# Where a one-core transformer kernel computes a convolution's filter, splits its weights and turns its heads: a rearranged instruction order on one Trainium2 core

## The reference

```python
for l in range(DEPTH):
    xn = rmsnorm(x, norm_mix[l])
    # a: chunked attention with a relative bias; b: difference of two softmaxes;
    # c: attention to the keys that an indexer picks (top_k of its scores)
    y = g[:, :, 0] * (o_a @ w_up_a[l]) + g[:, :, 1] * (o_b @ w_up_b[l]) + g[:, :, 2] * (o_c @ w_up_c[l])
    x = x + y @ w_out[l]
    x = x + memory_cross_attention(rmsnorm(x, norm_cross[l]), mem_n, w_q_x[l], w_kv_x[l], w_o_x[l])
    x = x + swiglu(rmsnorm(x, norm_ffn[l]), w_gu[l], w_down[l])
```

```python
def hyena_filter(length, fw1, fb1, fw2, fb2, fw3, fb3, fw4, freq):
    h = jnp.sin(freq * (emb @ fw1 + fb1))
    h = jnp.sin(freq * (h @ fw2 + fb2))
    h = jnp.sin(freq * (h @ fw3 + fb3))
    h = (h @ fw4).astype(jnp.float32)
    h_fwd = h[:, :HY_WIDTH] * window
    h_bwd = h[:, HY_WIDTH:] * window
```

## Time and profile before

| | us |
|---|---|
| runs, median (lowest to highest) | 3005.87 (3005.4 to 3010.86) |
| the profiled execution | 2997.0 |
| its span | 2995.2 |
| PE busy in it | 2914.2 (97%) |
| VectorE (DVE) busy | 1969.0 (66%) |
| ScalarE (ACT) busy | 1273.9 (43%) |
| GpSimd (POOL) busy | 226.4 (8%) |
| mean granted clock of TensorE | 0.991 |

### The profile page before, as it was taken

The page is one execution under the profiler, slowest core; times in us unless marked ns, Lnnn a source line. Parts: engine busy times, 40 slices in busy tenths (PEclk is TensorE's granted clock), DMA queues, the critical chain, the costliest instruction groups (busy, mean ns, idle before and its releaser), DMA issues.

```text
span 2995.2 us, 55989 instructions
## 1 busy us (share of the span) xinstructions
PE 2914.2 (97%) x23366; PEld 2765.4 (92%) x23366; DVE 1969.0 (66%) x3288; ACT 1273.9 (43%) x2199; POOL 226.4 (8%) x304
## 2 busy tenths in 40 slices
PE   8999899999999999999999999999999998999999
PEld 7889799988998999999977899999999998887899
DVE  6676688567768867767586666665666655335655
ACT  4455554445555463222545352223522234235543
POOL 1311100132101000000011200000000001001000
PEclk9999999999999999999999999999999999999999
DMA  6435377543546745554231234444345443342464
GB/s 210 132 121 173 121 246 236 173 126 110 169 145 207 247 159 197 183 180 157 93 109 43 75 113 162 151 143 138 127 162 168 142 144 97 113 148 92 148 197 135
DMA packets 246240, 448.49 MB, mean 150 GB/s; under 512 B 14739, under 2 KB 88356, under 8 KB 245348
## 3 DMA queue, kind: packets, MB, share of 16 engines
q1 hardware_dynamic: 239072, 430.79, 44.5%
q10 hardware_dynamic: 6916, 14.12, 1.4%
HBM read 442.75 MB, written 1.05 MB: 148 GB/s over the span
## 4 chain that ended last, share of the span: by engine, by line
PE 86%; DVE 8%; ACT 4%; issue 2%; POOL 0%; DMA 0%; ACTq 0%; SPq 0%; DVEq 0%; POOLq 0%
PE ps L1390 67%; DVE split L2202 3%; PE ps L1468 2%; PE ps L1469 2%; PE ps L1470 2%; ACT split L1876 1%; PE ps L1575 1%; PE ps L1340 1%; DVE A L2199 1%; PE ps L1764 1%; PE ps L1290 1%; PE ps L1599 1%; ACT A L1926 1%; ACT AR L1923 1%; DVE AR L2202 1%
## 5 line engine op out<-in xcount | busy, mean ns | idle before, releaser
L1390 PE MATMUL ps<-AR,split 128*128 128x256 f32 x18528 | 2211.4, 280 | 20.7 <-POOL AR L2762 5.3
L1390 PEld LDWEIGHTS ps<-AR,split 128*128 128x128 f32 x18528 | 2158.7, 189 | 64.0 <-issue 30.8
L2202 DVE TENSOR_TENSOR split<-raw,split 128x1024 fp32r<-128x1024 f32 (+2 forms) x728 | 810.0, 1150 | 546.6 <-ACT split L1876 540.1
L1876 ACT ACTIVATE split<-raw 128x1024 fp32r<-128x1024 f32 (+2 forms) x728 | 686.7, 987 | 761.9 <-PE ps L1390 670.0
L2487 DVE SCALAR_TENSOR_TENSOR junk<-A,cb 128x1024 bf16<-128x1024 f32 x144 | 175.6, 1220 | 42.0 <-DMA A<-w_modT 39.3
L2202 DVE TENSOR_TENSOR AR<-A,AR 128x256 fp32r<-128x256 f32 (+2 forms) x292 | 144.7, 496 | 48.7 <-ACT A L1926 25.8
L2487 DVE SCALAR_TENSOR_TENSOR A<-A,cb 128x1024 f32<-128x1024 f32 x144 | 175.3, 1218 | 0.0
L2755 POOL TENSOR_TENSOR A<-A 128x256 f32<-128x256 f32 x54 | 41.0, 759 | 1586.4 <-ACT A L1895 1583.4
L1948 ACT ACTIVATE AR<-A 128x256 fp32r<-128x256 f32 (+1 forms) x132 | 68.4, 526 | 193.4 <-DVE A L2326 193.4
L2199 DVE SCALAR_TENSOR_TENSOR A<-A,ps 128x256 f32<-128x256 f32 (+1 forms) x196 | 95.0, 505 | 49.3 <-ACT A L1944 44.7
L1944 ACT ACTIVATE A<-ps 128x256 f32<-128x256 f32 (+1 forms) x132 | 62.6, 490 | 128.4 <-PE ps L1390 125.8
(11 more groups left out here) (267 smaller groups left out, 2525.0 us busy)
## 6 DMA issues: line engine op xcount, KB each, us to landing
A<-w_modT SPq DMA_DIRECT2D x144, 512.0 KB, 4.5
raw<-w_in SPq DMA_DIRECT2D x120, 512.0 KB, 4.3
raw<-w_gu SPq DMA_DIRECT2D x80, 512.0 KB, 4.8
raw<-ffn_a_in SPq DMA_DIRECT2D x80, 512.0 KB, 4.5
raw<-ffn_b_in SPq DMA_DIRECT2D x80, 512.0 KB, 4.5
raw<-ret_in SPq DMA_DIRECT2D x48, 512.0 KB, 4.4
raw<-w_down SPq DMA_DIRECT2D x44, 512.0 KB, 4.7
raw<-ffn_a_out SPq DMA_DIRECT2D x44, 512.0 KB, 4.4
```

What stands on the lines that cost most here:

```text
L1390: mm = e.matmul(out[:, s:s + NT], wt[:, c, m_], xs(k0 + c, a + s, a + s + NT), start=first and part + s == 0, stop=last and part == 2 and ...
L1876: e.activation(hi, self.raw_view(q), ACT.Copy).then_inc(*self.mark(("w hi", q)))
L2202: return self.e.tensor_tensor(out, v, hi.bitcast(F32), ALU.subtract)
```

## The change

It moves work in the walk, and changes a few waits and banks:

- The start: VectorE no longer waits for x at first (`await_inputs` does it after the first norm's sums), its first half of a weight is split after the reciprocal, 14 warm-up matmul calls for 8, single halves prepared behind chunks 1, 3 and 5.
- The indexer of layer 0 takes PSUM banks 4, 6, 7, 0 in place of 0, 1, 2, 3.
- The fence before the first attention becomes `await_first`, which waits for the banks of q, k and v of attention a; the wait for the second attention's values moves from `await_second` to the first `diff_values`.
- In the cross attention weights are split at side steps 2 and 3 (not 4 and 6), the split at step 7 is dropped, and the root table is loaded at step 4.
- The silu of c is made in two halves in layer 0's output projection.
- The filter network: its loads go into layer 0's gate product, its three layers and sines into layer 0's down product, its taps and VectorE's end into the norm behind and layer 1's start, the products of its transform into layer 1's feed-forward norm and down product. The even stage keeps none of it.
- The retention: the second half of q's parts (m > 3) is exchanged by DMA as k's are; weights for it are split at steps 5 and 6 of the crossing, and the context's chunks start at step 7 and not 5.
- In an attention pipeline, put-off halves are no longer split in the rounds in which no new unit starts and at most two are live.

```diff
@@ pipeline
-                if put_off:
+                if put_off and (new or parts > 2):
                     self.split_beside(at, parts)
@@ cross_steps
-            if c == 3 and early:
-                self.prepare(AHEAD, True)
+            if c == 3:
+                self.prepare_beside()
+            if early and c in (5, 6):
+                self.prepare(AHEAD, c == 5)
                 self.asked -= 1
-            elif c == 3:
-                self.prepare_beside()
...
-            if c > 4:
+            if c > (6 if early else 4):
                 next(ctx)
@@ walk, the start
-        self.prepare_first()
-        self.warm(8)
+        if self.name != "dve":
+            self.prepare_first()
+        self.warm(14)
         self.norm_sums(n0)
+        if self.name == "dve":
+            self.prepare_first()
+        self.await_inputs()
@@
-then=lambda c: c in (2, 4) and self.prepare_behind(c // 2 - 1))
+then=lambda c: c in (1, 3, 5) and self.prepare_behind(c // 3, c == 3))
@@ layer_one, after the cross attention
+        if l == 1:
+            self.filter_product(0, 0)
         self.next_sums(nf, 0)
+        if l == 1:
+            self.filter_product(0, 1)
...
-            if n == 12 and l == 0:
-                self.mod_start()
+            if l == 0 and n < 96 and n % 16 == 12:
+                self.load_filter(n // 16)
@@ layer_one, down
+            if l == 0 and k in (0, 5, 10):
+                self.filter_layer(k // 5)
+            if l == 0 and k in (4, 9, 14):
+                self.filter_sine(k // 5)
+            if l == 1 and k == 2:
+                self.filter_product(1, 0)
+                self.filter_product(1, 1)
+            if l == 1 and k == 3:
+                self.filter_spectra(1)
         if l == 0:
             h = self.H1("h mix 1")
-            self.next_norm(nn, self.xl, h, gain=self.cl("norm_mix", 8, 8))
+            self.filter_tap("forward", 0, 6)
+            self.next_sums(nn, 1)
+            self.filter_tap("backward", 0, 7)
+            self.norm_spread(nn["name"], [nn])
+            self.filter_tap("forward", 1, 4)
+            h.norm = nn["name"]
+            self.norm_apply(nn, self.xl, h, gain=self.cl("norm_mix", 8, 8))
+            self.filter_end(0)
@@ beside_cross
+            if k in (2, 3):
+                self.prepare(0, k == 2)
+                self.asked -= 1
             if k == 4:
                 self.await_memory_values(l)
-            if k in (4, 6):
-                self.prepare(0, k == 4)
-                self.asked -= 1
-            if k == 5:
                 self.load_roots()
-            if k == 7:
-                self.prepare_beside(True)
@@ mixing
-        run(first_a, self.indexer(...))
+        run(first_a)
+        if l == 1:
+            self.filter_tap("backward", 1, 6)
+            self.filter_end(1)
+        run(self.indexer(...))
...
-        self.fence()
-        self.fence(("act",))
+        self.await_first(l)
@@ the output projection
+            if l == 0 and k in (1, 9):
+                self.mod_start(k // 8)
@@ odd
-self.project_t("q r", w, 0, 1024, h, lambda m, f: self.axial(..., m, rawb, tmpb), ...)
+self.project_t("q r", w, 0, 1024, h, lambda m, f: self.axial(..., m, rawb, tmpb, moved=m > 3), ...)
@@ TensorE.indexer
-        waits = [self.K.take(f, PROJ) for f in fills]
+        waits = [self.K.take(f, (4, 6, 7, 0) if l == 0 else PROJ) for f in fills]
@@ TensorE
+    def await_first(self, l):
+        for m in range(4):
+            for v in ("qa", "ka"):
+                self.e.wait_ge(*self.after(("free", ((v, l), m))))
+        for m in range(2):
+            self.e.wait_ge(*self.after(("free", (("va", l), 0, m))))
+
+    def filter_product(self, kind, m):
+        f = (("even", "odd")[m], "filter spectrum", kind)
+        out = self.fresh(f, (6 + m,))
+        self.e.wait_ge(*self.after("fdft"))
+        self.e.wait_ge(*self.after(("filter taps", m)))
+        o = FDFT + kind * 256 + m * P
+        self.e.matmul(out[:, :], self.A[:, o:o + P], self.taps(2 * kind + m), start=True, stop=True).then_inc(*self.mark(("full", f)))
@@ ScalarE.axial
-        if ctx is not None:
+        if moved:
             e.wait_ge(*self.after(("raw", f)))
             e.dma_start(dst[0:64, :], raw[64:128, :])...
             e.dma_start(dst[64:128, :], raw[0:64, :])...
```

More of the change, by code:

```diff
@@ L589, in first_block @@
         h.norm = "first"
-        self.norm_apply(n0, self.xl, h, self.cl("norm_mix", 0, 8), then=lambda c: c in (2, 4) and self.prepare_behind(c // 2 - 1))
+        self.norm_apply(n0, self.xl, h, self.cl("norm_mix", 0, 8), then=lambda c: c in (1, 3, 5) and self.prepare_behind(c // 3, c == 3))
         self.await_tables()
@@ L606, in first_block, with prepare_behind @@
         return h
-    def prepare_behind(self, ahead):
-        self.prepare(ahead)
+    def prepare_behind(self, ahead, part):
+        self.prepare(ahead, part)
         self.asked -= 1
@@ L740, in context_norm @@
             yield
+        yield
         self.norm_sums(N)
@@ L1001, in hyena_spectra @@
         for kind in range(2):
-            self.filter_spectra(kind)
-            yield
-        for kind in range(2):
             self.spectra(0, kind)
@@ L1257, in nothing @@
         pass
[L1259 removed]
+    start = finish = await_inputs = warm = split_memory = await_tables = prepare_first = norm_feed = norm_sums = norm_spread = keep = add_x_out = add_mod_out = add_set_out = nothing
     silu = gated = gated_low = gate = up = rotary = index_twice = index_weights = index_score = nothing
@@ L1623, in await_second @@
             self.e.wait_ge(*self.after(("rotated", ((v, l), 3))))
-        for m in range(2):
-            self.e.wait_ge(*self.after(("free", (("vb", l), 0, m))))
     def diff_values(self, name, pt, nk, vs, o, ptb, kt):
@@ L1629, in diff_values @@
         out = self.fresh(f, BESIDE[2])[:, 0:P]
+        if name[2] == name[3] == 0:
+            for m in range(2):
+                self.e.wait_ge(*self.after(("free", (("vb", name[1]), 0, m))))
         self.e.wait_ge(*self.after(("pt", name)))
@@ L1710, in forward @@
             self.e.matmul(out[:, :], self.A[:, o:o + P], src(m), start=True, stop=True).then_inc(*self.mark(("full", (part, *f))))
-    def filter_spectra(self, kind):
-        self.e.wait_ge(*self.after("dft"))
-        self.forward(("filter spectrum", kind), lambda m: self.taps(2 * kind + m), kind, lambda m: ("filter taps", m))
     def spectra(self, s, kind):
         ZT = 18432
+        if s == kind == 0:
+            self.e.wait_ge(*self.after("dft"))
         self.forward(("spectrum", kind, s), lambda m: self.A[:, ZT + (2 * s + m) * 512:ZT + (2 * s + m + 1) * 512], kind, lambda m: ("free", ("z turn", 2 * s + m)))
@@ L1830, in load_lambda @@
     def load_lambda(self, l):
+        if l == 1:
+            self.e.wait_ge(*self.after(("filter taps", 1)))
         if l == 0:
@@ L2063, in await_projected @@
         self.e.wait_ge(*self.after(rsb.freed(7)))
-        self.e.wait_ge(*self.after(("filter taps", 1)))
     def normed(self, f, dst, gain, sqb, rsb):
@@ L2095, in filter_spectra @@
     def filter_spectra(self, kind):
-        self.keep(("even", "filter spectrum", kind), self.A[:, HS + (2 * kind + 1) * 512:HS + (2 * kind + 2) * 512], 1)
+        self.keep(("even", "filter spectrum", kind), self.taps(2 * kind), 1)
     def spectra(self, s, kind):
@@ L2116, in axial @@
         raw = self.A[:, o:o + NT]
-        e.activation(raw, self.bank(f)[:, 0:NT], ACT.Copy, scale=scale).then_inc(*self.mark(("raw", f), *([("free", f)] if ctx is not None else [])))
-        if ctx is not None:
+        e.activation(raw, self.bank(f)[:, 0:NT], ACT.Copy, scale=scale).then_inc(*self.mark(("raw", f), *([("free", f)] if moved else [])))
+        if moved:
             e.wait_ge(*self.after(("raw", f)))
@@ L2187, in start, with await_inputs @@
     def start(self):
-        for v in ("cols", "eps", "x0", "x1", "x2", "x3"):
+        for v in ("cols", "eps"):
+            self.e.wait_ge(*self.after(v))
+    def await_inputs(self):
+        for v in ("x0", "x1", "x2", "x3"):
             self.e.wait_ge(*self.after(v))
@@ L2589, in filter_spectra @@
     def filter_spectra(self, kind):
-        self.both_halves(("filter spectrum", kind), kind, HS + 2 * kind * 512)
+        e, f = self.e, ("filter spectrum", kind)
+        low, high, odd = self.taps(2 * kind), self.taps(2 * kind + 1), self.bank(("odd", *f))[:, :]
+        e.wait_ge(*self.after(("free", ("even", *f))))
+        e.wait_ge(*self.after(("full", ("odd", *f))))
+        if kind == 0:
+            e.tensor_tensor(high, low, odd, ALU.subtract).then_inc(*self.mark(("frequencies", f, 1)))
+        else:
+            e.tensor_tensor(high, odd, low, ALU.subtract).then_inc(*self.mark(("frequencies", f, 1)))
+        e.tensor_tensor(low, odd, low, ALU.add).then_inc(*self.mark(("free", ("odd", *f)), ("frequencies", f, 0)))
     def spectra(self, s, kind):
-        self.both_halves(("spectrum", kind, s), kind, ZS[s] + 2 * kind * 512)
```

(2 more changed lines are left out.)

158 lines of the change are left out of this document (72 added, 86 removed).

## The result

| | before | after |
|---|---|---|
| median of 10 runs (lowest to highest), us | 3008.97 (2998.41 to 3022.84) | 2992.48 (2972.42 to 3000.16) |
| ratio to before | | 0.9933, 95% interval 0.9907 to 0.9959 |
| the profiled execution's span, us | 2995.2 | 2995.8 |
| granted clock, mean | 0.991 | 0.989 |

In these runs the change is faster, by 20 us of 3009 as the ratio goes (12 to 28), where 29.5 were forecast; 2992.5 lies in the range of 2957 to 2994, near its upper end. The two profiled executions show no difference at all. So the first question is what hides it there.

A forecast was written before the change was run, and what follows sets the result against it. PE, busy 2914.2 of 2995.2 us, was taken as the bound, with gains only in its waits and half clock. Terms summed to -31.5, with +2 for new waits -29.5: 3005.87 to 2976 us, range 2957 to 2994.

The forecast's parts named there:

- rival 1: Whole kernel: waits are displaced, each term gives only its low end, -3.5 us, half of that way -12; chance 0.11.
- F: Layer 0's gate product: moving the silu of c to the output projection removes PE's 3.4 us wait, -2.9 us.
- G: Filter network: the even stage loses 13.3 us on PE, 6.1 come back elsewhere, -7.2 us.
- H: Start of the retention layer: earlier weight splits and half of q's parts turned by DMA, -8 us.
- E: Cross attention's tail, both layers: earlier splits and one dropped shorten PE's waits for POOL, -4.4 us.
- A, B: Kernel start and layer 0's indexer banks: PE's waits for the sums and for DVE's copies shrink, -2.0 us each.
- C, D: Fence before the first attention narrowed, diff attention's wait for values moved to first use: -1.5 us each.
- I: PE's clock, whole kernel: some half-clock loss goes where waits go, -2 us, between -6 and +2.
- J: Last two attention pipeline rounds: no put-off splits there, 0 us, between -2 and +2.
- Rival 3: Filter network: PE waits at each of 13 hand-offs, 23 us lost at 1.75 each, 3015 at 3 each; chance 0.04.
- The estimate of -13 by the clock: Whole kernel, skill's rule taken strictly: about half of the 27 us lost to clock returns, -13 in place of -2.
- The DMA's fixed time: Retention: about 2.0 us per transfer would stall DVE for each uncovered turned part, up to 8 us, leaving no gain there.

The follow-up runs named there:

- the second set: Another set of runs of the same two kernels, before and after, nothing edited: ratio 0.9981 (0.9958 to 1.0004).
- same_again: The changed kernel once more, nothing edited: median 3002.22 us, ratio to before 0.9981, profiled span 3004.4 us.
- before_again: The kernel before once more, nothing edited: profiled span 2998.3 us.

## Why the prediction was right, and by which steps it was too large

The direction and the range held, the range with some luck. Its upper end, 2994, came from rival 1's -12, called half of the way from the forecast to -3.5. Half of that way is -16.5, or 2989, and 2992.5 lies above it; and the second set's 0.9981, put on 3005.87, would be 3000. Of the sum of -31.5 some -13.3 bare is what the traces show, and the clock gave nothing or took 5. Undone one at a time, the parts come to 6.3, 2.2, 0.4, 0.2 and 1.3, or 10.4 us; the 3 us to 13.3 are not assigned and lie within what these readings leave open. Of the signs named, the waits of B and F went, the even stage with the long convolution is 14.9 shorter and down with what follows 3.9 longer. POOL's wait did not vanish, and the retention's stretch, the half clock at new places and PE's wait on copies behind DMA issues were as the signs of being wrong had it. The steps:

- **G, the filter network: right.** -7.2 forecast, -6.3 measured (-5.4 against the second profile). Both sides were low: 13.3 against 15.0 gained and 6.1 against 8.7 given back. What came back beyond the sum is the loads (0.7), the first layer's wait of 1.0 in down, and the spectrum matmuls in layer 1's norm, 1.2, which I took to be hidden. On PE layers and products cost what the rows had said (the four taps 5.5 us in place of 3.7); the middle line is the retention's rotations, for H:

```profile
L1727 PE MATMUL ps<-fil,A 128*128 128x512 f32 x8 | 4.0, 602 | 0.0
...
L1764 PE MATMUL ps<-A,base 128*128 128x256 f32 x8 | 2.0, 392 | 0.7 <-ACT A L2146 0.7
L1710 PE MATMUL ps<-A 64*64 64x256 f32 (+1 forms) x6 | 1.9, 396 | 1.0 <-issue 1.0
```

- **H, the retention: mis-sized, -8 against -2.4.** The step that failed is the count of ScalarE's queue to 2519. After, ScalarE and its queue, then PE:

```profile
2514.71 1.99 ACT L1906 ACTIVATE split<-raw 128x1024 fp32r<-128x1024 f32 x2
2516.61 0.59 ACT L1953 ACTIVATE AR<-A,mods,gsc 128x256 fp32r<-128x256 f32 x1
...
2517.59 0.36 ACT L2146 ACTIVATE A<-ps 128x256 f32<-128x256 f32 x1
2517.98 0.59 ACTq L2149 DMA_DIRECT2D A<-A  x1
2518.60 0.61 ACTq L2150 DMA_DIRECT2D A<-A  x1
2519.26 0.60 ACT L1953 ACTIVATE AR<-A,mods,gsc 128x256 fp32r<-128x256 f32 x1 [1.31 <-DVE AR L2235]
...
2520.26 0.36 ACT L2146 ACTIVATE A<-ps 128x256 f32<-128x256 f32 x1
...
2521.82 0.60 ACT L1953 ACTIVATE AR<-A,mods,gsc 128x256 fp32r<-128x256 f32 x1 [1.20 <-DVE AR L2235]
...
2522.81 0.36 ACT L2146 ACTIVATE A<-ps 128x256 f32<-128x256 f32 x1
```

```profile
2507.62 10.06 PE L1400 MATMUL ps<-AR,split 128*128 128x256 f32 x72 [2.63 <-DVE A L2684]
2523.32 8.86 PE L1400 MATMUL ps<-AR,split 128*128 128x256 f32 x51 [5.64 <-ACT A L2146]
```

PE has done q's last matmul at 2517.7 and stands 5.6 us, until 2523.3; what releases it is the third of four copies (L2146), the one that ends at 2523.2. The first starts at 2517.6, behind two splits and a context chunk, and between the copies stand two DMA issues of 0.5 to 0.6 us and a context chunk each time. I had counted what ScalarE does, and not what it waits for: 1.7, 0.9 and 1.8 us for DVE's sums (L2312) between 2505 and 2514, and the 1.3 and 1.2 shown. DVE makes the chunks' low parts, the rotations and the weights' low halves in one queue and so ends the step before each of them. The rotations that went (8 of 16, 2.0 us left of 6.7) are more than the whole gain of 2.4. The stretch from q's last 96 matmuls to k's first is 24.5 us, from 28.4; 18 were forecast.

- **E, the cross attention: the wait was exchanged, -4.4 against -0.4.** The term took the wait for POOL and did not say what the splits are put ahead of:

```profile
352.86 1.23 DVE L2235 TENSOR_TENSOR split<-raw,split 128x1024 fp32r<-128x1024 f32 x1 [0.91 <-ACT split L1906]
354.00 0.75 DVE L2440 TENSOR_REDUCE small<-ps 128x1 f32<-128x256 f32 x2
...
355.00 0.16 DVE L2453 RECIPROCAL small<-small 128x2 f32<-128x2 f32 x1
```

```profile
355.19 1.09 PE L1300 MATMUL ps<-base,A 128*128 128x128 f32 x4 [2.46 <-DVE small L2453]
...
362.59 1.61 PE L1400 MATMUL ps<-AR,split 128*128 128x256 f32 x12 [0.82 <-POOL AR L2801]
```

The second low half, at 352.86, stands before DVE's maxima of the last unit (354.00); their reciprocal ends at 355.16, and PE has stood 2.46 us for it. The POOL side of the step was right to the decimal (0.9 each for cast and subtract): 2.6 became 0.82.

- **F, the silu: exchanged too, -2.9 against about 0 bare.** The gate product's stage is 4.4 shorter, as forecast and a little more. The term took the clock at 1.00 behind this wait from one execution; in two others it was 0.50, so some executions gain by the clock what the bare reading does not show. I gave the halves cover in the output projection. DVE there:

```profile
308.90 1.22 DVE L2232 SCALAR_TENSOR_TENSOR cb<-A,cb 128x1024 f32<-128x1024 f32 x1
...
310.83 1.22 DVE L2232 SCALAR_TENSOR_TENSOR cb<-A,cb 128x1024 f32<-128x1024 f32 x1
...
312.76 2.35 DVE L2235 TENSOR_TENSOR split<-raw,split 128x1024 fp32r<-128x1024 f32 x2
...
315.37 0.42 DVE L2232 SCALAR_TENSOR_TENSOR X<-ps,X 128x256 f32<-128x256 f32 x1
```

The two products of 1.22 us push the pair of low halves to 312.76, and the sum that frees PE's first bank to 315.37; PE waits 2.4 for it. The cover holds for PE's time (22 us), not for DVE's before the first banks come free.

- **A, B: -4.0 forecast, -0.5 bare and -1.7 by clock** in the first profile; undoing them cost 3.6, 3.4 of it by clock. The waits of 3.8 and 2.6 us are gone; the bound that I gave for more warm-ups, that they delay the sums, is near what happened: the 28 matmuls (14 calls) end at 10.2 us, and the sums start at 10.07, where they started at 10.75.
- **C, D: -3.0 forecast, -2.2 measured**, in the two stages in which they stand. The fence's wait did not go away whole: 0.7 us at 45 and 1.0 at 77 remain.
- **I, the clock: -2 forecast, 0 to +5.** Half clock lies at other places in each execution of one kernel, and sums to 56 and 66 us in before's two profiles and to 66 and 66 in after's: none of it came back.
- **J: nothing** that a stage shows, as forecast.
- **The rival of displaced waits** (1) had the mechanism for E, F and half of H; it gave -12 us. In the traces the bare gain of 13.3 stands nearer to it than to the forecast. The ratio of the first set (20 us) stands between the two, that of the second (6 us) below both.
- **Rival 3**, PE waiting at each of the filter's hand-offs: it waits 1.0 us in all for them.
- **The estimate of -13 by the clock**, which the prediction took from the Trainium skill (TensorE: Matmul & The Clock Gate, Part 1: The HAM clock gate): no profile shows such a gain. But the rule itself, that idleness throttles, is borne out better than the earlier trace rows let it appear, by the half clock behind the gate product's wait in two of three profiles.
- **The DMA's fixed time**, 2.0 us by the Trainium skill (DMA: Bandwidth & Descriptors, Anatomy of one DMA). The section states it for transfers that GpSimd issues; these go out on ScalarE's queue, and the trace of after has 2.5 us from issue to landing (median of 24, 64 KB each). DVE stood 2.67 us for the first turned part of q, until 2523.48, but PE had been released at 2523.3 by a copy, so it cost PE nothing that this trace shows. The kernel with the turn by DMA alone was the better of the two.

What stays open: whether after's true gain is nearer 6, 13 or 20 us. The ratios of two sets say 20 (12 to 28) and 6 (-1 to 13) and the traces 13.3 less some clock. The two intervals overlap from 12 to 13 us, 0.4%.

## What to carry to other kernels

A wait removed is worth the wait less the next one, and the next one is found by asking what the moved instruction now stands ahead of on its own engine: a split ahead of a maximum, a product ahead of the sum that frees the first bank. Cover has to be counted on the engine that is moved to, up to the first thing that the bound engine needs from it. Where the same work can run at two speeds, line two traces up by the k-th instruction and compare by stage; a stage that no edit touches tells how fine the reading is. And take two traces of each kernel before resting a term on what the clock did in one.

## What the runs showed of the hardware that was not expected

- The same stream of weight loads and matmuls of 256 columns, at a granted clock of 1.00 and with no wait, runs at 113.3 or at 117.8 ns from start to start, and stays at one for up to 850 us. Over 13 profiles of nearly the same work 233 to 592 of 771 blocks were wide, 25 to 64 us. Some 90 blocks were wide in all of them, mostly short spells before 890 us and most of the time from 1570 to 1760 us; some 60 were narrow in all; the rest changed from profile to profile. 38 small matmuls of 128 x 128 weights did not switch it, the filter's with weights of 17 x 64 did, in ten of ten profiles. What settles it was not found. Between after and same_again it is 7.7 of 8.6 us; that it makes most of the runs' spread of 28 us for one kernel is likely but not shown, since most runs have no trace.
- The same wait of PE brings half clock in one execution and not in the next: 3.44 us with 1.00 behind it in before, 3.45 us with 0.50 in before_again. Stretches at half clock moved between executions of one kernel.
- POOL's small casts of 128 x 128 take 0.29 us alone and 1.18 beside DVE's subtract; with the subtract moved away all four of the layer took 0.29.
